# Splits before squares, a later memory norm, and alpha x written by ScalarE: three edits to a two-block transformer kernel

## The chip, the cores and the metric

The kernel runs on one core of a Trainium2 chip. TensorE (PE) multiplies matrices into eight PSUM banks, VectorE (DVE) and ScalarE (ACT) work elementwise, GpSimd (POOL) does next to nothing here, and SyncE (SP) issues nearly all DMAs. The metric is device time in microseconds (us) of one execution; lower is better.

## What is computed

Batch 1, 256 tokens, width 1024, all in float32. The first block is a chain of residual steps, the second a chain of post-norm steps. Cut from the reference:

```python
# first block
h = h + 0.5 * swiglu(rms_norm(h, g_ffn1), w_ffn1_gate, w_ffn1_up, w_ffn1_down)   # 1024 -> 2816 -> 1024
u = rms_norm(h, g_mix) @ w_in            # two kinds of attention over u, then @ w_out, added to h
h = h + 0.5 * swiglu(rms_norm(h, g_ffn2), ...)
h = h + sigmoid(rms_norm(h, g_ple_in) @ w_ple_gate + b) * rms_norm(p @ w_ple_proj, g_ple_out)
# second block, two layers l = 0, 1
mem_n = layer_norm(mem, mem_ln_g, mem_ln_b)
y = hybrid_ab_mixer(x, ...) if l == 0 else multiscale_pool_mixer(x, ...)
x = layer_norm(ALPHA * x + y, ln_mix_g[l], ln_mix_b[l])
y = memory_cross_attention(x, mem_n, w_q, w_k, w_v, w_o)
x = layer_norm(ALPHA * x + y, ln_xa_g[l], ln_xa_b[l])
y = (silu(x @ w_gate) * (x @ w_up)) @ w_down
x = layer_norm(ALPHA * x + y, ln_ffn_g[l], ln_ffn_b[l])
```

## The kernel before

**The weight stream.** All weights are cut into blocks of 128 x 1024 numbers (512 KB), numbered in the order in which PE uses them. SP loads block b into one of four raw buffers (`w_raw`) as soon as the low part of block b - 4 is made. ACT copies it, rounded, to `w_hi` (`part_hi`, L529), DVE subtracts to get `w_lo` (`part_lo`, L1046), and PE multiplies three times per tile, hi x hi, hi x lo and lo x hi (`three`, L1852 to L1854). A block of a feed-forward is 12 matmuls of 512 columns. The ring of `w_hi` and `w_lo` also has four places, so ACT may split block b + 4 when PE is done with block b: `behind(b)` is that step on ACT and on DVE. The activations are split in the same way (`x_hi` and `x_lo`, `h_hi` and `h_lo`).

**What sets the order.** Each engine's program is written out by hand, in the order in which it runs; semaphores join them. An engine never takes a later instruction first.

**A feed-forward** (`token_ffn(f, b0)`, f = 0 to 3) goes over the 2816 hidden columns in six steps n. Step 0 runs blocks G0 (gate, four blocks) and U0 (up, four). Each later step n runs G(n) with `turn_h(n-1)` in its middle (the hidden part turned from tokens to features), the four down blocks D(n-1), and U(n). Gate products stand in banks 0 and 1, up products and turned parts in 2 and 3, the sum of the down products in 4 to 7. ACT does the sigmoid (`sig`), DVE the two products (`gated`, `hidden`).

**The start.** PE multiplies ones to pass the time (22 matmuls, L2251), turns x (L1972), and begins G0. ACT does: split of weight block 0, half 0 of `x_hi` (L554, with waits for DVE's `x_lo`, L1068), squares of half 0 (L561), split of block 1, half 1 of `x_hi`, squares of half 1, splits of blocks 2 and 3. DVE follows with `w_lo` and `x_lo`, and makes the token rms (`token_rstd`, L1125 on), for which it needs all squares, between `w_lo` of block 2 and of block 3.

**The memory norm** lies inside the first feed-forward. `mem_tok` is loaded from ACT's DMA queue at the end of the start. DVE's `memory_stats` (L1168 to L1178) stands right behind `gated(0)`, ACT's `memory_norm` (L576) in U0, PE's `turn_memory` (L2003, 16 transposes into banks 4 to 7) behind `turn_h(0)`, ACT's `memory_gain` (L582) behind it; PE waits for the gain before the first down blocks. The split of the result (`memory_hi`, `memory_lo`) and `rope_tables` stand in step 2.

**The last two feed-forwards** (f = 2, 3) take x from a layer norm. `ln_norm` leaves the normalised x, tokens on partitions, in `xs[:, :, 1, :]`; PE turns it (`ln_turn`, L1910, token half t = 0 then 1), ACT applies gain and bias (`ln_x`, L668). Of G0, the first two blocks are split ahead, and `token_turns` runs all of G0 for t = 0, then for t = 1, with `ln_turn(v, 1)` behind the third block of t = 0. ALPHA x enters the output sum on PE: `residual` (L1938) multiplies x by ALPHA times the identity, eight float32 matmuls a call, behind the down blocks of steps 1 and 2. `T_BANK` says which banks the turns use.

**The end.** After the last block PE turns t = 0 and t = 1 of the last norm; ACT applies gain and bias to feature chunks 0 to 3 of both halves, DVE (L1836) to 4 to 7, and SP stores the four quarters (L504).

## Time and profile before

| | us |
|---|---|
| median of 3 runs (1311.31 to 1312.6) | 1312.11 |
| the profiled execution, its device time | 1311.42 |
| its span, first to last instruction | 1309.6 |
| PE busy | 1283.6 |
| DVE busy | 855.8 |
| ACT busy | 654.8 |

The profiled execution's time is 1.8 us over its span, and 0.7 us under the median. The mean granted TensorE clock is 0.992 of full speed. In the views, L12 is line 12 of the kernel; a row of the timeline has its start, its length, the engine, the line, and in brackets the idle time before it with what ended it. xN at a row's end is a run of N like instructions told as one.

### The profile page before, as it was taken

To read this page: it belongs to the slowest core of one execution; us is meant where nothing else is said; L and a number is where in the kernel's file an instruction comes from. 1 tells how busy PE (TensorE), PEld (TensorE's weight loads), DVE (VectorE), ACT (ScalarE), POOL (GpSimd) and SP (SyncE) were. 2 spreads that over 40 slices of the span, in tenths; PEclk is the share of its full clock that TensorE was granted. 3 is DMA by queue.
4 is the path that set the end of the run, shared out by engine and by line. 5 is a ranking of instruction groups with operands and counts; after the bars stand their busy time and mean duration, and the time that the engine had idled before them with its cause. 6 is when DMAs were issued, how large, how long until landed. Compare 5 with 4: busy or idle time off the path is not lost.

```text
span 1309.6 us, 17902 instructions
## 1 busy us (share of the span) xinstructions
PE 1283.6 (98%) x7108; PEld 1113.8 (85%) x7108; DVE 855.8 (65%) x1435; ACT 654.8 (50%) x987; POOL 5.4 (0%) x7
## 2 busy tenths in 40 slices
PE   8999999999999999999999999999999999999997
PEld 7888888897788888899889897888888997888886
DVE  5665557878667565678988765654557665555555
ACT  5554446657474444453535645543445654634442
POOL 0000000000000000000000000000001000000000
PEclk9999999999999999999998999999999999999998
DMA  8555555552355555544424532655554442555551
GB/s 278 185 183 189 192 177 194 174 165 81 105 178 191 185 186 191 178 145 162 147 95 137 184 131 94 216 179 179 186 191 146 164 143 81 193 177 180 189 191 51
DMA packets 61570, 215.82 MB, mean 165 GB/s; under 512 B 6576, under 2 KB 9904, under 8 KB 61232
## 3 DMA queue, kind: packets, MB, share of 16 engines
q1 hardware_dynamic: 61056, 213.15, 49.2%
q10 hardware_dynamic: 432, 1.54, 0.4%
q8 instruction: 56, 0.92, 0.3%
q14 instruction: 26, 0.21, 0.1%
HBM read 213.62 MB, written 1.05 MB: 164 GB/s over the span
## 4 chain that ended last, share of the span: by engine, by line
PE 86%; DVE 10%; ACT 2%; DMA 1%; issue 1%; SPq 0%; DVEq 0%; ACTq 0%
PE bank L1852 25%; PE bank L1854 25%; PE bank L1853 25%; DVE arena L1669 3%; DVE w_lo L1046 2%; PE bank L2051 1%; PE bank L1938 1%; PE bank L1874 1%; PE bank L2189 1%; PE bank L2149 1%; DMA w_raw<-weights_d 1%; PE bank L2160 1%; ACT w_hi L529 1%; DVE tokst L1325 0%; PE bank L2181 0%
## 5 line engine op out<-in xcount | busy, mean ns | idle before, releaser
L1046 DVE TENSOR_TENSOR w_lo<-w_raw,w_hi 128x1024 fp32r<-128x1024 f32 x383 | 467.1, 1225 | 355.3 <-ACT w_hi L529 353.9
L529 ACT ACTIVATE w_hi<-w_raw 128x1024 fp32r<-128x1024 f32 x383 | 404.1, 1059 | 500.5 <-PE bank L1854 479.9
L1852 PE MATMUL bank<-w_hi,x_hi 128*128 128x512 f32 (+2 forms) x992 | 373.3, 376 | 7.2 <-DVE w_lo L1046 6.5
L1854 PE MATMUL bank<-w_hi,x_lo 128*128 128x512 f32 (+2 forms) x992 | 367.8, 371 | 0.0
L1853 PE MATMUL bank<-w_lo,x_hi 128*128 128x512 f32 (+2 forms) x992 | 367.7, 371 | 0.0
L1852 PEld LDWEIGHTS bank<-w_hi,x_hi 128*128 128x128 f32 x992 | 187.6, 189 | 40.6 <-DVE w_lo L1046 7.6
L1854 PEld LDWEIGHTS bank<-w_hi,x_lo 128*128 128x128 f32 x992 | 187.6, 189 | 31.6
L1853 PEld LDWEIGHTS bank<-w_lo,x_hi 128*128 128x128 f32 x992 | 187.8, 189 | 30.4
L1852 PE MATMUL bank<-w_hi,h_hi 128*128 128x512 f32 (+1 forms) x364 | 142.3, 391 | 0.0
L1853 PE MATMUL bank<-w_lo,h_hi 128*128 128x512 f32 (+1 forms) x364 | 141.3, 388 | 0.0
L1854 PE MATMUL bank<-w_hi,h_lo 128*128 128x512 f32 (+1 forms) x364 | 141.3, 388 | 0.0
L1852 PEld LDWEIGHTS bank<-w_hi,h_hi 128*128 128x128 f32 x364 | 68.3, 188 | 14.7 <-DVE h_lo L1064 1.2
L1854 PEld LDWEIGHTS bank<-w_hi,h_lo 128*128 128x128 f32 x364 | 68.3, 188 | 14.0
L1853 PEld LDWEIGHTS bank<-w_lo,h_hi 128*128 128x128 f32 x364 | 68.4, 188 | 13.5
L1852 PE MATMUL bank<-x_hi,w_hi 128*128 128x256 f32 x256 | 74.3, 290 | 2.3 <-DVE arena L1698 0.9
L1853 PE MATMUL bank<-x_lo,w_hi 128*128 128x256 f32 x256 | 72.4, 283 | 0.0
L1854 PE MATMUL bank<-x_hi,w_lo 128*128 128x256 f32 x256 | 72.4, 283 | 0.0
L1852 PEld LDWEIGHTS bank<-x_hi,w_hi 128*128 128x128 f32 x256 | 49.0, 192 | 3.1 <-DVE arena L1698 1.1
L1669 DVE SCALAR_TENSOR_TENSOR arena<-arena,prm 128x256 f32<-128x256 f32 x120 | 50.0, 477 | 0.5
L1853 PEld LDWEIGHTS bank<-x_lo,w_hi 128*128 128x128 f32 x256 | 49.1, 192 | 0.2
L1854 PEld LDWEIGHTS bank<-x_hi,w_lo 128*128 128x128 f32 x256 | 49.1, 192 | 0.0
L1874 PE MATMUL bank<-xs,w_raw 128*128 128x256 f32 x192 | 43.0, 381 | 0.2 <-DVE xs L1633 0.2
(311 smaller groups left out, 1461.1 us busy)
## 6 DMA issues: line engine op xcount, KB each, us to landing
w_raw<-weights_d SPq DMA_DIRECT2D x395, 512.0 KB, 3.3
arena<-weights_d SPq DMA_DIRECT2D x4, 512.0 KB, 6.1
arena<-late_d SPq DMA_DIRECT2D x1, 1056.0 KB, 5.8
xs<-x_d SPq DMA_DIRECT2D x2, 512.0 KB, 6.1
kv_mem<-mem_d ACTq DMA_DIRECT2D x1, 1024.0 KB, 7.5
out_d<-xs SPq DMA_DIRECT2D x4, 256.0 KB, 2.8
cst<-cst_d SPq DMA_DIRECT2D x1, 671.0 KB, 10.4
arena<-pT_d ACTq DMA_DIRECT2D x1, 256.0 KB, 2.6
```

Source lines behind the costliest of these rows:

```text
L529: nc.scalar.activation(w_hi[:, slot(b), :], w_raw[:, b % RAW, :], ACT.Copy).then_inc(hi_ready, 1)
L1046: nc.vector.tensor_tensor(w_lo[:, slot(b), :], w_raw[:, b % RAW, :], w_hi[:, slot(b), :].bitcast(F32), ALU.subtract).then_inc(lo_ready, 1)
L1669: ins = nc.vector.scalar_tensor_tensor(conv[:, c, :], src, w, conv[:, c, :], ALU.mult, ALU.add)
L1852: nc.tensor.matmul(out, wh, xh, start=start, stop=False, skip_group_check=True)
L1853: nc.tensor.matmul(out, wh, xl, start=False, stop=False, skip_group_check=True)
L1854: return nc.tensor.matmul(out, wl, xh, start=False, stop=stop, skip_group_check=True)
L1874: ins = nc.tensor.matmul(out, w_raw[:, b % RAW, k * P:(k + 1) * P], x[:, k, 0, :], start=k == 0, stop=k == TILES - 1)
L1938: nc.tensor.matmul(PB[banks[t]][:, c % 4 * P:c % 4 * P + P], xs[:, c, 0, t * P:(t + 1) * P], res_i, start=False, stop=False, skip_group_ch ...
L2051: ins = nc.tensor.transpose(PB[2 + k][:, at:at + P], hf[:, t, (2 * k + j) * P:(2 * k + j + 1) * P], ident)
L2149: ins = nc.tensor.matmul(half(n % 2, t), xq[:, 2 * h + k, t * P:(t + 1) * P], k_mem[l][:, 2 * h + k, :], start=k == 0, stop=k == 1)
L2160: ins = nc.tensor.transpose(PB[2 + n % 2][:, k * S + t * P:k * S + (t + 1) * P], e_buf(n)[:, 0, t, k * P:(k + 1) * P], ident)
L2189: ins = nc.tensor.matmul(o[:, c * S:(c + 1) * S], v_mem[l][:, k, at:at + P], pt_buf(n)[:, k, :], start=k == 0, stop=k == 1)
```

## The change

1. **The start.** ACT splits weight blocks 1, 2 and 3 and all of `x_hi` first, then makes all four squares. DVE makes `w_lo` of block 3 before `token_rstd(0)`.
2. **Loads.** `mem_tok` is now loaded by SP, ahead of block 8, and `cst` ahead of block 12 (it was issued behind the first four blocks).
3. **The memory norm.** `memory_stats` moves behind the second block of D(0), `memory_norm` behind the second block of U(1). `turn_memory` comes in two halves of eight transposes, into banks 2 and 3, in the middle of D(1) and of D(2), with a wait for `f_hl`; ACT's gain comes in two halves behind it, and PE waits for each half before U(2) and U(3). `rope_tables` moves to step 3, the split of the result to step 4.
4. **ALPHA x of the last two feed-forwards.** PE's `residual` is gone there. DVE makes x in token form from the normalised x: four products with rows of the gain and four sums with rows of the bias (`residual_rows`), before `gated(0)`. ACT writes ALPHA times the four parts into banks 4 to 7 (`residual_in`), behind `sig(0)` and before the split of G1's first block; the first down blocks wait for it and add to it. The rows (1 MB for each layer) are loaded by SP ahead of G1's first block. The turns of t = 1 of the norms ahead (v = 6, 9) use banks 2 and 3 instead of 4 and 5, so PE waits there until ACT has read t = 0.
5. **The end.** ACT applies gain and bias to all eight chunks of t = 0 before its part of norm t = 1, then to chunks 0 to 3 of t = 1; DVE does only chunks 4 to 7 of t = 1.
6. In `weighted`, a start flag is set once for both halves of a bank.

```diff
-        T_BANK = {5: (0, 2, 4, 5), 6: ((2, 3), (4, 5)), 7: (0, 1, 4, 5), 8: (4, 5, 0, 1), 9: ((2, 3), (4, 5)),
+        T_BANK = {5: (0, 2, 4, 5), 6: ((2, 3), (2, 3)), 7: (0, 1, 4, 5), 8: (4, 5, 0, 1), 9: ((2, 3), (2, 3)),
...
-            sp.dma_start(cst[:], cst_d).then_inc(cst_in, 16)
             for b in range(RAW, NB):
+                if b == 2 * RAW:
+                    sp.dma_start(mem_tok, mem_d).then_inc(mem_in, 16)
+                if b == 3 * RAW:
+                    sp.dma_start(cst[:], cst_d).then_inc(cst_in, 16)
...
+                if b in (FIRST["ffn3"] + 6, FIRST["ffn4"] + 6):
+                    l = 0 if b < FIRST["ffn4"] else 1
+                    sp.wait_ge(t_ps, NH + XA_HEADS * (l + 1))
+                    sp.dma_start(ln_rows, row_d[l]).then_inc(row_in, 16)
...
+            def residual_in(f):
+
+                for h in range(2):
+                    for t in range(2):
+                        act.wait_ge(xt_ready, XT[f + 2] + 2 * h + t + 1)
+                        nc.scalar.activation(quarters(PB[Y_BANK[V_OUT[f]][2 * h + t]][:, :]), x_part(h, t, 1), ACT.Copy, scale=ALPHA
+                                             ).then_inc(y_set, 1)
...
                 sig(0)
+                if f >= 2:
+                    residual_in(f)
...
                 for i in range(AHEAD if f >= 2 else 0, 4):
                     behind(b0 + ffn_place("G", 0, i))
+                if f >= 2:
+                    residual_rows(f)
                 gated(0)
-                if f == 0:
-                    memory_stats()
...
+            def residual_rows(f):
+
+                dve.wait_ge(row_in, 16 * (f - 1))
+                dve.wait_ge(xt_ps, 16 + 4 * LN[V_IN[f]] + 4)
+                parts = [(x_part(h, t, 1), [quarters(ln_rows[:, k, h * HALF:(h + 1) * HALF]) for k in range(2)])
+                         for h in range(2) for t in range(2)]
+                for x, (g, _) in parts:
+                    mark(nc.vector.tensor_tensor(x, x, g, ALU.mult))
+                settle()
+                for x, (_, b) in parts:
+                    nc.vector.tensor_tensor(x, x, b, ALU.add).then_inc(xt_ready, 1)
...
+                if t and v != 10:
+                    pe.wait_ge(xn_ready, XN[v] + DC)
...
+                        if f >= 2 and n == 0 and jp == 0:
+                            pe.wait_ge(y_set, 4 * (f - 2) + 2 * h + 2)
...
                     for i in range(4):
-                        if f == 0 and n == 1 and i < 2:
-                            pe.wait_ge(mem_g, 4 * i + 4)
+                        if f == 0 and n in (2, 3) and i == 2:
+                            turn_memory(n - 2)
                         down(b1 + ffn_place("D", n - 1, i), n - 1, i // 2, i % 2)
-                    if f >= 2 and n < 3:
-                        residual(Y_BANK[V_OUT[f]][2 * n - 2:2 * n], n - 1)
                     up(n)
```

**On ACT at the start** (x_hi and w_hi are the rounded parts, the rows that read xs into xs are the squares). Before:

```order
L529 ACTIVATE w_hi<-w_raw 128x1024
L554 ACTIVATE x_hi<-bank,prm 128x256 x4
L561 ACTIVATE xs,tokst<-xs 128x4x128 x2
L529 ACTIVATE w_hi<-w_raw 128x1024
L554 ACTIVATE x_hi<-bank,prm 128x256 x4
L561 ACTIVATE xs,tokst<-xs 128x4x128 x2
L529 ACTIVATE w_hi<-w_raw 128x1024 x2
```

and after:

```order
L538 ACTIVATE w_hi<-w_raw 128x1024
L563 ACTIVATE x_hi<-bank,prm 128x256 x4
L538 ACTIVATE w_hi<-w_raw 128x1024
L563 ACTIVATE x_hi<-bank,prm 128x256 x4
L538 ACTIVATE w_hi<-w_raw 128x1024 x2
L570 ACTIVATE xs,tokst<-xs 128x4x128 x4
```

All four squares now stand behind the splits of blocks 1, 2 and 3.

**On DVE at G0 of the third feed-forward** (the last rows of the splits of x, the splits of U0's blocks, `gated(0)`, the splits of G1's first three, `hidden(0)`; the fourth feed-forward reads alike). Before:

```order
L1064 TENSOR_TENSOR x_lo<-xs,x_hi 128x2x128 x4
L1046 TENSOR_TENSOR w_lo<-w_raw,w_hi 128x1024 x3
L1225 TENSOR_TENSOR arena<-bank,arena 128x512 x2
L1046 TENSOR_TENSOR w_lo<-w_raw,w_hi 128x1024 x3
L1225 TENSOR_TENSOR arena<-bank,arena 128x512 x2
```

and after:

```order
L1082 TENSOR_TENSOR x_lo<-xs,x_hi 128x2x128 x4
L1064 TENSOR_TENSOR w_lo<-w_raw,w_hi 128x1024 x3
L1343 TENSOR_TENSOR xs<-xs,arena 128x4x128 x4
L1346 TENSOR_TENSOR xs<-xs,arena 128x4x128 x4
L1243 TENSOR_TENSOR arena<-bank,arena 128x512 x2
L1064 TENSOR_TENSOR w_lo<-w_raw,w_hi 128x1024 x3
L1243 TENSOR_TENSOR arena<-bank,arena 128x512 x2
```

Eight instructions stand before `gated(0)` and the splits of G1.

**On ACT at the end** (the norm's parts read bank and tokst, gain and bias read bank and prm). Before:

```order
L609 ACTIVATE h_hi<-bank 128x512
L529 ACTIVATE w_hi<-w_raw 128x1024
L660 ACTIVATE xs<-bank,tokst 128x4x128 x2
L668 ACTIVATE xs<-bank,prm 128x128 x8
L165 UNCONDITIONAL_BRANCH
```

and after:

```order
L626 ACTIVATE h_hi<-bank 128x512
L538 ACTIVATE w_hi<-w_raw 128x1024
L679 ACTIVATE xs<-bank,tokst 128x4x128
L687 ACTIVATE xs<-bank,prm 128x128 x8
L679 ACTIVATE xs<-bank,tokst 128x4x128
L687 ACTIVATE xs<-bank,prm 128x128 x4
L165 UNCONDITIONAL_BRANCH
```

The eight chunks of t = 0 now stand between the two parts of the norm, and four rows are new on ACT (DVE has four fewer).

## Rows read from the trace of the kernel before

**Rows 1.** From the page: busy time, share and instructions of PE, PEld, DVE, ACT

```profile
PE 1283.6 (98%) x7108; PEld 1113.8 (85%) x7108; DVE 855.8 (65%) x1435; ACT 654.8 (50%) x987; POOL 5.4 (0%) x7
```

**Rows 2.** Timeline of PE, start to 39 us: four rows with idle time before them

```profile
15.15 0.50 PE L1852 MATMUL bank<-w_hi,x_hi 128*128 128x512 f32 x1 [1.31 <-DVE w_lo L1046]
...
19.93 0.50 PE L1852 MATMUL bank<-w_hi,x_hi 128*128 128x512 f32 x1 [1.77 <-DVE w_lo L1046]
23.64 0.50 PE L1852 MATMUL bank<-w_hi,x_hi 128*128 128x512 f32 x1 [0.65 <-DVE w_lo L1046]
38.41 0.47 PE L1852 MATMUL bank<-w_hi,x_hi 128*128 128x512 f32 x1 [0.87 <-DVE w_lo L1046]
```

**Rows 3.** Timeline of ACT and DVE, 11 to 41 us

```profile
11.56 0.62 ACT L561 ACTIVATE xs<-xs 128x512 f32<-128x512 f32 x1
12.79 1.05 ACT L529 ACTIVATE w_hi<-w_raw 128x1024 fp32r<-128x1024 f32 x1
13.87 1.23 DVE L1046 TENSOR_TENSOR w_lo<-w_raw,w_hi 128x1024 fp32r<-128x1024 f32 x1 [1.68 <-ACT w_hi L529]
17.58 3.89 ACT L529 ACTIVATE w_hi<-w_raw 128x1024 fp32r<-128x1024 f32 x4
19.80 0.15 DVE L1125 TENSOR_TENSOR tokst<-tokst 128x2 f32<-128x2 f32 x1
22.36 1.23 DVE L1046 TENSOR_TENSOR w_lo<-w_raw,w_hi 128x1024 fp32r<-128x1024 f32 x1
24.30 3.49 DVE L1046 TENSOR_TENSOR w_lo<-w_raw,w_hi 128x1024 fp32r<-128x1024 f32 x3
31.56 2.46 DVE L1168 BATCH_NORM_STATS2 tokst<-kv_mem 128x6 f32<-128x512 f32 x4
37.05 3.49 DVE L1046 TENSOR_TENSOR w_lo<-w_raw,w_hi 128x1024 fp32r<-128x1024 f32 x3
```

**Rows 4.** Timeline of PE around one `residual` of the third feed-forward

```profile
855.22 1.95 PE L1938 MATMUL bank<-res_i,xs 128*128 128x128 f32 x16
856.92 0.48 PE L1852 MATMUL bank<-w_hi,x_hi 128*128 128x512 f32 x1
```

**Rows 5.** Timeline of DVE and PE at U0 and G1 of the third feed-forward

```profile
821.67 2.59 DVE L1046 TENSOR_TENSOR w_lo<-w_raw,w_hi 128x1024 fp32r<-128x1024 f32 x2 [0.45 <-ACT w_hi L529]
821.67 0.39 PE L1852 MATMUL bank<-w_hi,x_hi 128*128 128x512 f32 x1
826.38 1.23 DVE L1046 TENSOR_TENSOR w_lo<-w_raw,w_hi 128x1024 fp32r<-128x1024 f32 x1
832.55 0.39 PE L1852 MATMUL bank<-w_hi,x_hi 128*128 128x512 f32 x1
```

**Rows 6.** Timeline, first feed-forward: four DVE, four ACT instructions of 512 elements, all in SBUF

```profile
82.96 2.49 DVE L1064 TENSOR_TENSOR m_lo<-kv_mem,m_hi 128x512 fp32r<-128x512 f32 x4
...
81.45 2.19 ACT L589 ACTIVATE m_hi<-kv_mem 128x512 fp32r<-128x512 f32 x4
```

**Rows 7.** DMA issues by line: KB each, median us from issue to landing

```profile
arena<-late_d SPq DMA_DIRECT2D x1, 1056.0 KB, 5.8
```

**Rows 8.** Timeline, third feed-forward: ACT's last of t = 0, and PE's turn of t = 1

```profile
811.02 0.79 ACT L668 ACTIVATE xs<-bank,prm 128x128 f32<-128x128 f32 x2
813.67 1.04 PE L1910 MATMUL bank<-ident,xs 128*128 128x128 f32 x8
```

**Rows 9.** The end: timeline of ACT, PE, DVE; landing of the stores; a stretch of 1 us

```profile
1302.62 2.90 ACT L668 ACTIVATE xs<-bank,prm 128x128 f32<-128x128 f32 x8
1302.77 1.92 PE L1910 MATMUL bank<-ident,xs 128*128 128x128 f32 x8 [2.98 <-ACT xs L660]
...
1304.73 1.36 DVE L1836 TENSOR_SCALAR xs<-bank,prm 128x128 f32<-128x128 f32 x4 [0.83 <-PE bank L1910]
...
DMA to landing us min/median/max: 2.4/2.8/3.1
...
1306.00:1307.00 1.00, 0.00 (x0) 0.00 (x0) 0.09 (x1) 0.00 (x0) 0.00 (x0) 0.50 0.99 286
```

The columns of the last row are: stretch, us, busy us of PE, PEld, DVE, ACT and POOL, granted clock, DMA share, GB/s.

More of the change, by code:

```diff
@@ L577, in memory_norm, with memory_gain @@
                                              bias=ln_m[:, t:t + 1]).then_inc(mem_xn, 1)
-            def memory_gain():
-                for c in range(DC):
+            def memory_gain(h):
+                for c in range(4 * h, 4 * h + 4):
                     act.wait_ge(mem_t, c // 2 + 1)
-                    nc.scalar.activation(mem_f[:, c, :], half(4 + c // 2, c), ACT.Identity, scale=col("mem_g", c),
+                    nc.scalar.activation(mem_f[:, c, :], half(2 + c // 2 % 2, c), ACT.Identity, scale=col("mem_g", c),
                                          bias=col("mem_b", c)).then_inc(mem_g, 1)
@@ L1019, in _ @@
             token_ffn(3, FFN4)
+            ln_x(10, 0, 0, DC)
             ln_norm(10, 1)
-            for t in range(2):
-                ln_x(10, t, 0, 4)
+            ln_x(10, 1, 0, 4)
         @block.vector
@@ L1266, in token_ffn @@
                     hidden_lo(n - 1)
-                    if f == 0 and n == 2:
+                    if f == 0 and n == 3:
+                        rope_tables()
+                    if f == 0 and n == 4:
                         memory_lo()
-                        rope_tables()
                     if f == 1 and n == 1:
@@ L1278, in token_ffn @@
                         behind(b1 + ffn_place("D", n - 1, i))
+                        if f == 0 and n == 1 and i == 1:
+                            memory_stats()
                         if f == 1:
@@ L2041, in up @@
                         pe.wait_ge(f_hl, FFN_LO_ALL * f + 2 * n)
+                    if f == 0 and n in (2, 3):
+                        pe.wait_ge(mem_g, 4 * (n - 1))
                     for i in range(DC * FFN_W[n] // BLK):
@@ L2087, in token_ffn @@
                     turn_h(n - 1)
-                    if f == 0 and n == 1:
-                        turn_memory()
                     gate(n, 2)
@@ L2189, in weighted @@
                             ins = nc.tensor.matmul(o[:, c * S:(c + 1) * S], v_mem[l][:, k, at:at + P], pt_buf(n)[:, k, :],
-                                                   start=k == 0, stop=k == 1)
+                                                   start=c == 0 and k == 0, stop=k == 1, skip_group_check=True)
                 ins.then_inc(o_ps, 1)
@@ L2700 @@
               "prm": small_parameters(x), "ident": np.eye(P, dtype=np.float32), "cst": constants(),
-              "late": np.concatenate([pool_bands(), np.broadcast_to(x["pool_scale_2"].reshape(1, D), (P, D))], 1), "weights": np.ascontiguousarray(weight_stream(x))}
+              "late": np.concatenate([pool_bands(), np.broadcast_to(x["pool_scale_2"].reshape(1, D), (P, D))], 1),
+              "ln_rows": np.stack([np.broadcast_to(np.stack([x[f"ln_xa_{k}_2"][l] for k in "gb"]), (P, 2, D)) for l in range(2)]), "weights": np.ascontiguousarray(weight_stream(x))}
     nc = bacc.Bacc("TRN2", target_bir_lowering=False, num_devices=1)
```

52 lines of the change are left out of this document (26 added, 26 removed).

## The prediction

> **What bounds the kernel now.** I read the page's busy times first: PE is busy for 1283.6 of 1309.6 us, DVE for two thirds, ACT for half [rows 1]. So an edit gains only where it shortens PE's own work, one of PE's few waits, or the two ends of the program. PE's timeline comes next, for its idle time: four waits for DVE's `w_lo`, 4.6 us together, lie in the first 39 us [rows 2]. In the middle of a feed-forward PE needs 832.55 - 821.67 = 10.88 us for the four blocks of U0 [rows 5], so 2.72 for a block, while DVE needs 1.23 and ACT 1.05 for its share of one [rows 3]. There each has some 1.5 us to spare per block.
>
> **The start.** Squares of one half cost ACT 1.23 us (11.56 to the split that follows at 12.79) [rows 3]. With them behind:
> - Block 1 is split from 11.56 instead of 12.79, DVE makes its `w_lo` from 12.64 (was 13.87) to 13.87, and PE, through with block 0 at 13.84, starts it at 13.9 instead of 15.15.
> - Block 2 is split two pairs of squares earlier, at 17.58 - 2.46 = 15.1. Its `w_lo` ends at 15.1 + 1.05 + 1.25 = 17.4 and PE starts it at 17.5, having waited 0.6 (it needs 3.0 us for a block here: 15.15 to 19.93, less the idle 1.77 [rows 2]).
> - Block 3 is split from 16.1, its `w_lo` is there at 18.6, and PE starts it at 20.5, when it is through with block 2. That was 23.64.
> - Block 4 is late next. The squares now run from 17.1 to 19.6. The rms behind them takes DVE 22.36 - 19.80 = 2.56 us, to 22.2; the small instructions up to the next split take 24.30 - 22.36 less 1.13, the pitch of a split, so 0.8. Its `w_lo` then runs from 23.0 to 24.25 [rows 3]. PE is free at 20.5 + 2.8 = 23.3 and waits 1.0. Before, it started this block at 26.4 (five blocks lie between 23.64 and 38.41 - 0.87, so 2.78 each). 2.1 us are gained here.
>
> The memory norm's move takes away the last wait of 0.87 before block 8 [rows 2], since `memory_stats` no longer stands ahead of its split: I expect that `w_lo` by 30.1, and PE asks for it at 24.3 + 4 x 2.78 = 35.4. The start of block 8 moves from 38.41 to 35.4: **3.0 us**. The loads that SP takes over are no bound here: `mem_tok` is issued at 18.6 behind weight block 7, and a load of 1056 KB landed in 5.8 us [rows 7]; blocks 6 and 7, issued at 17.4 and 18.6, are needed on PE only from 29.9 on.
>
> Further on the norm's pieces lie beside full PE work. The longest, DVE's `memory_stats` (31.56 to 37.05, 5.5 us [rows 3]), now stands behind a split while PE has about four blocks, 10.9 us, before it needs the next one; split, statistics and split take 1.1 + 1.2 + 5.5 + 1.2 = 9.0. Covered by 1.9; if that cover were gone, it would cost what is over. Two breaks of PE's stream for eight transposes in place of one for 16 cost 0.1. Nothing for the rest.
>
> **ALPHA x.** One `residual` costs PE 856.92 - 855.22 = 1.70 us, and the matmul behind it restarts 0.08 late (0.48 long [rows 4] instead of 0.39 [rows 5]): 1.78, four times: **7.1 us**, all on PE, which has no wait in these stretches.
>
> What comes in is beside PE, but on engines that PE follows. At the third feed-forward DVE is through with U0's last split at 821.67 + 2.59 = 824.26 [rows 5]. Four instructions of 512 elements in SBUF take 2.49 us together, 0.62 each [rows 6]; four products and four sums take 4.95, to 829.2. ACT must wait for each sum. Its last copy starts at 829.2; a write of 512 elements from ACT to PSUM is nowhere in this trace, so I bound it by the copy within SBUF, 0.6 [rows 6], and by no time at all, and take 0.6: 829.8. Only then does ACT split G1's first block (1.05), and DVE makes `w_lo` by 829.8 + 1.05 + 1.25 = 832.1. PE asks for it at 832.55 [rows 5]. So it fits by 0.4 us, where before it was 826.38 + 1.23, 4.9 us early. `gated(0)`, which with its wait fills at most 824.26 to 826.38 now, 2.1 us [rows 5], is done by 831.3 even so, before ACT's split of G1 is used. The next splits follow at 833.3 and 834.5 and are asked for at 835.3 and 838.0: the lag is worked off. I take **0** and keep 0 to 1.5 us for each of the two feed-forwards.
>
> A rule of the Trainium skill speaks against this. "VectorE: DVE Perf Modes", in the section on the TRN2 errata, gives (N + 151)/0.96 ns for a float32 tensor_tensor, 691 ns at 512; four times that is 2.76, and the four of [rows 6] took 2.49, because each starts before the one ahead of it has ended. If each of the eight took the page's time one after the other, they would take 5.5 us, and by it PE would wait 0.15 us in each feed-forward and the sum would be 0.3 us worse.
>
> The wait before the turn of t = 1 costs nothing: ACT ends t = 0 at 811.8, PE turns at 813.67 [rows 8]. Behind it on PE stands G0's last block, which needs x parts that come later anyway. The rows' load, 1 MB, is issued near 814 and lands near 820 by [rows 7]; DVE wants it at 824.2, and blocks queued behind it on SP are wanted later still.
>
> **The end.** PE's turn of t = 0 ends at 1302.77 - 2.98 = 1299.8. ACT, idle until the norm's second part (it ends where the eight of L668 begin, 1302.6), can take t = 0 from about 1299.3 on: eight chunks at 0.36 [rows 9] end at 1302.2. The norm's part on ACT starts 0.3 later, and so do PE's turn and DVE's last four chunks, which end at 1304.73 + 1.36 + 0.3 = 1306.4. A loss of 0.3. Against it stand the stores: now all four are issued within 2.4 us and the DMA engines are full at 286 GB/s [rows 9]; 1 MB at that rate is 3.7 us. Issue to landing is 2.4 us at best and 3.1 at worst; I take the worst for the last store now and the best after the change, when half the data has left before 1304. 0.3 lost, 0.6 to 0.7 gained: **0.3 us** gained, between 0.4 lost and 0.8 gained.
>
> **Sum.** 3.0 + 7.1 - 0.1 + 0.3 = 10.3, and the span becomes 1299.3, the profiled execution 1301.1 (1.8 over it). The median before is 0.7 above its profiled execution, so I forecast 1301.8 us for the median.
>
> **The rivals.**
> - *The start gives less.* DMA engines are near full in the first 15 us, and if blocks 6 and 7, with `mem_tok` behind them, land later than I think, or the rms chain stretches, PE waits again before block 8. For it: DVE's chain is the new bound with nothing to spare at block 4. Against: what is issued at 17.4 has 12 us. It would leave 1 of the 3.0 us: 1304.
> - *ACT and DVE at G1 are late.* The margin of 0.4 us comes out of seven steps in a row, each waiting for another engine. If each of DVE's eight takes a third longer than the rows' 0.62, by the way in which its operands lie, the chain is 1.6 us longer, and a slower last copy adds up to 0.4, and PE waits 1.2 to 1.6 us, twice: 1304 to 1305. Against: the sources are in SBUF, as in [rows 6].
> - *The first weights come earlier too*, with `cst` gone from behind them, and PE starts by up to 1.5 us sooner: 1300.3. Against: `cst` was issued last, behind what PE waits for.
> - *Slower.* DVE waits in order for the rows of gain and bias; behind it stand `gated(0)` and every split, so PE stands still soon after. The load reaches 10.3 us of loss in all, and so no gain, when PE waits 5.2 us in each feed-forward: the rows would have to land at 824.2 + 0.4 + 5.2 = 829.8, nearly 16 us after issue, where a load of the size took 5.8 [rows 7]. At 18 us after issue the kernel would take 1317.
> - *The change doesn't do what it says:* if PE's time for `residual` was cover for ACT or DVE, removing it uncovers them. In these steps both wait for PE by some 1.5 us per block, so I give it no more than half of the 7.1 us: 1305.
>
> **How the numbers follow.** Forecast 0.68, within 1300.0 to 1303.5 (the bounds of start, 2 to 3.6, and end). Start gives less 0.09, late at G1 0.12, earlier weights 0.05, slower 0.02, uncovered engines 0.04. A measurement of this kernel tells about 0.2%, 2.6 us, from no change. Range 1299.6 to 1305: it leaves out part of the earlier weights, the deep end of the stalls and the slower case. Faster by over 0.2% holds in all but the slower case and the worst sums of the others: 0.96; within 0.2% 0.02; slower 0.02.
>
> **What would show it.** Start: PE's row with a wait for `w_lo` near 24.3 with 1.0 us of idle, and none near 38; block 8 at 35.4. ALPHA x: no rows of the residual after the third feed-forward starts, no wait of PE at G1's first block, and the `w_lo` before it done less than 1 us ahead. End: PE's last turn 0.3 later after the last block than now, last store landing in 2.4 to 2.5 us. I am wrong if PE shows waits of more than 1 us at the two G1, or new ones in D(1) to U(3) of the first feed-forward.

## The result, and the profile after

The changed kernel took 1298.72 us in the median of four runs (1298.31 to 1301.42), the kernel before, beside it, 1311.71: a ratio of 0.9906 with an interval of 0.9891 to 0.9920. That is 13.0 us less, and 3.1 less than the 1301.8 that I forecast; it lies just below my range. All executions of the study together give less: 1310.5 in the median of 79 executions of before (1309.0 to 1312.7), and 1299.9 in that of 14 of after (1298.3 to 1301.4), 10.7 apart.

The profiled execution took 1301.42 us, with a span of 1299.6; I had written 1301.1 and 1299.3. From the page of after, beside [rows 1]:

```profile
PE 1273.5 (98%) x7044; PEld 1104.1 (85%) x7044; DVE 864.3 (67%) x1447; ACT 660.8 (51%) x999; POOL 5.7 (0%) x7
```

PE is busy for 10.1 us less, DVE and ACT for 8.5 and 6.0 more, and PE still bounds. The waits of PE's timeline in the first 280 us of after, where [rows 2] had four:

```profile
17.23 0.50 PE L1883 MATMUL bank<-w_hi,x_hi 128*128 128x512 f32 x1 [0.55 <-DVE w_lo L1064]
24.00 0.50 PE L1883 MATMUL bank<-w_hi,x_hi 128*128 128x512 f32 x1 [1.02 <-DVE w_lo L1064]
```

These are blocks 2 and 4, forecast at 17.5 with 0.6 and at 24.3 with 1.0, and the wait at 38.41 is gone: between the second of these and 293 us PE has no wait over 0.1 us. DVE, then ACT, then DVE and PE again at G1 of the third feed-forward in after, where [rows 5] had `w_lo` of G1 at 826.38:

```profile
818.80 2.59 DVE L1064 TENSOR_TENSOR w_lo<-w_raw,w_hi 128x1024 fp32r<-128x1024 f32 x2 [0.45 <-ACT w_hi L538]
821.30 2.49 DVE L1343 TENSOR_TENSOR xs<-xs,arena 128x512 f32<-128x512 f32 x4
823.83 2.50 DVE L1346 TENSOR_TENSOR xs<-xs,arena 128x512 f32<-128x512 f32 x4
826.25 1.28 DVE L1243 TENSOR_TENSOR arena<-bank,arena 128x512 f32<-128x512 f32 x2
827.98 3.50 DVE L1064 TENSOR_TENSOR w_lo<-w_raw,w_hi 128x1024 fp32r<-128x1024 f32 x3 [0.45 <-ACT w_hi L538]
```

```profile
824.56 2.41 ACT L605 ACTIVATE bank<-xs 128x512 f32<-128x512 f32 x4 [2.03 <-DVE xs L1346]
826.90 4.11 ACT L538 ACTIVATE w_hi<-w_raw 128x1024 fp32r<-128x1024 f32 x4
```

```profile
829.69 0.39 PE L1883 MATMUL bank<-w_hi,x_hi 128*128 128x512 f32 x1
```

`w_lo` of G1's first block is there at 827.98 + 1.23 = 829.2, and PE takes it at 829.69 with no idle time in brackets. I had forecast a fit by 0.4 us; it fits by 0.5. DVE's row at 821.30 has no idle time either: the rows of gain and bias had landed, after 5.6 us.

What I had no line for is in the mixer of the second block. PE's timeline in after:

```profile
699.70 0.55 PE L1883 MATMUL bank<-m_hi,w_hi 128*128 128x256 f32 x1 [3.40 <-DVE w_lo L1064]
```

This wait of 3.40 us is not in the first profile of before. The stretches of 4 us around it (columns: stretch, us, busy us of PE, PEld, DVE, ACT and POOL, granted clock, DMA share, GB/s), first in before, then in after:

```profile
688.00:692.00 4.00, 4.00 (x36) 4.00 (x35) 3.89 (x6) 1.99 (x4) 0.00 (x0) 0.93 0.00 0
692.00:696.00 4.00, 4.00 (x20) 4.00 (x21) 3.59 (x18) 0.05 (x1) 0.00 (x0) 0.50 0.82 256
696.00:700.00 4.00, 4.00 (x26) 4.00 (x25) 3.65 (x18) 1.59 (x5) 0.00 (x0) 0.66 0.02 6
```

```profile
692.00:696.00 4.00, 4.00 (x36) 4.00 (x36) 3.66 (x18) 2.49 (x6) 0.00 (x0) 1.00 0.14 54
696.00:700.00 4.00, 0.60 (x4) 0.44 (x3) 3.72 (x12) 2.00 (x3) 0.00 (x0) 0.93 0.00 0
700.00:704.00 4.00, 4.00 (x24) 4.00 (x24) 4.00 (x10) 1.53 (x4) 0.00 (x0) 0.64 0.66 230
```

DVE is busy nearly throughout in both. A stretch of a few us in which the granted clock is at its lower level of 0.50 (1.2 GHz instead of 2.4) is called a fall below. In before, the falls came ahead of DVE's `w_lo`, and PE was 1.0 us late for it (it began the block at 703.96, and 684.33 + 18.65 = 702.98 is when DVE would have let it, see below). In after it ran at 1.00, came early, waited, and had the low clock behind the wait instead.

Measured between like rows of the two first profiles, the 10.0 us of span come from here: 0.27 at ACT's first split (8.00 to 7.73, the landing of block 0), 3.2 in the rest of the start, 3.2 and 3.6 in the two feed-forwards, and 0.3 at the end; 0.6 were lost in the mixer.

### The profile page after: what moved, and what is told of

The parts are those of the page before. It is cut to its first block, busy times and chain, and to the rows that moved or that the text cites. A ratio compares the mean times of both kernels' runs of the same rounds, so it can differ in the third digit from the quotient of the medians.

```text
span 1299.6 us, 17803 instructions
## 1 busy us (share of the span) xinstructions
PE 1273.5 (98%) x7044; PEld 1104.1 (85%) x7044; DVE 864.3 (67%) x1447; ACT 660.8 (51%) x999; POOL 5.7 (0%) x7
## 4 chain that ended last, share of the span: by engine, by line
PE 85%; DVE 11%; ACT 2%; issue 1%; DMA 1%; SPq 0%; DVEq 0%; ACTq 0%
PE bank L1883 25%; PE bank L1885 25%; PE bank L1884 25%; DVE arena L1702 3%; DVE w_lo L1064 3%; PE bank L2087 1%; PE bank L1905 1%; PE bank L2223 1%; PE bank L2183 1%; PE bank L1971 1%; DMA w_raw<-weights_d 1%; ACT w_hi L538 1%; PE bank L2194 1%; PE bank L2215 0%; ACT xs L570 0%
```

## The experiments

The open question was where a gain beyond my sum of 10.3 us came from. My first theory was the clock in the mixer, the rival a term of the sum that is too small.

**The parts.** After unedited; before with ALPHA x alone; after without it; after with the old order of the start; after with the old memory norm. Of the edits, the core lines:

```diff
# alpha_only: before, with (the two methods are those of the change)
+                if f >= 2:
+                    residual_in(f)
...
+                if f >= 2:
+                    residual_rows(f)
...
-                    if f >= 2 and n < 3:
-                        residual(Y_BANK[V_OUT[f]][2 * n - 2:2 * n], n - 1)
# no_alpha: after, with these undone
# no_start: after, with
             x_hi_of(0, 0, 4)
+            act.wait_ge(x_in[0], 32)
+            x_square(0, 0)
             part_hi(1)
             x_hi_of(0, 4)
+            act.wait_ge(x_in[1], 16)
+            x_square(0, 1)
             part_hi(2)
             part_hi(3)
-            act.wait_ge(x_in[0], 32)
-            x_square(0, 0)
-            act.wait_ge(x_in[1], 16)
-            x_square(0, 1)
...
             part_lo(2)
+            token_rstd(0)
             part_lo(3)
-            token_rstd(0)
# no_memory: after, with
                 gated(0)
+                if f == 0:
+                    memory_stats()
...
-                        if f == 0 and n in (2, 3) and i == 2:
-                            turn_memory(n - 2)
```

In no_memory the loads of `mem_tok` and `cst` are also back where they were.

> The changed kernel, unedited, to see what another execution of it looks like. Its profiled execution had a span of 1299.6 us, other executions 1296.5 and 1297.3. Theory 1, the clock: in the mixer of the second block (640 to 705 us) the granted TensorE clock fell in that execution (0.61 to 0.96 in eight us, 0.64 in four more), and where it does not fall the kernel ends some 2 to 3 us sooner; a profiled execution of 1296.5 us shows a clock of 1.00 from 640 to 705, and nothing else differs. Theory 2, a term of the sum was too small: 2.5 to 3 us are gained in every execution somewhere else (start, ALPHA x or end), and the timelines of the two executions differ by one wait that has nothing to do with the clock.

> Only the part on ALPHA x of the last two feed-forwards; start, memory norm and end as before. The sum says 7.1 us less than before. Theory 1: the mixer lies where it lay before, so its clock behaves as before, and it is 7 us and no more. Theory 2: 9.5 to 10 us if this part is the one that was priced too low.

> The change without the part on ALPHA x: the order at the start, the memory norm and the end are as changed. The sum says 3.0 + 0.3 - 0.1, so 3.2 us less than before. Theory 1: the mixer lies 3.3 us earlier, just as in the changed kernel, so the clock can do the same to it: 5.5 to 6.3 us less in most executions. Theory 2, with the start priced too low: the same 6 us in all executions, and the gain is seen ahead of 600 us.

> The changed kernel with the old order at the start (squares between the splits, rms before the low part of block 3). The sum says that this order is worth 2.1 of the 3.0 us of the start and the move of the memory norm 0.9, so the time is 2.1 us over that of the changed kernel. Theory 1: the mixer then lies 1.2 us earlier than before instead of 3.3, and the clock may fall in other executions than with the changed kernel, so 2 to 5 us over. Theory 2: 2.1.

> After, but with the memory norm where it was: memory_stats behind gated(0), the norm in U0, all 16 turns in step 1, its load from ACT's queue and cst behind the first four blocks. My sum says 0.9 of the start's 3.0 us goes with it (the wait before block 8), less 0.1 for the second break of the stream: 1300.7 beside 1299.9 of after. Rival: cst out of the way of the first weights makes block 0 arrive 0.3 us earlier, and this goes too: 1301.0, with ACT's first split back at 8.0 us instead of 7.73.

| kernel | median, us (executions) | ratio to before, 95% | against the before beside it, us |
|---|---|---|---|
| after_again | 1299.87 (1299.51 to 1300.55) | 0.9916 (0.9903 to 0.9930) | -11.3 |
| alpha_only | 1303.45 (1302.21 to 1304.63) | 0.9943 (0.9931 to 0.9955) | -7.7 |
| no_alpha | 1307.50 (1305.08 to 1307.80) | 0.9971 (0.9959 to 0.9982) | -3.7 |
| no_start | 1301.95 (1301.24 to 1302.63) | 0.9932 (0.9919 to 0.9944) | -9.2 |
| no_memory | 1300.72 (1299.42 to 1302.47) | 0.9927 (0.9915 to 0.9939) | -10.1 |

The parts add up: 7.7 + 3.7 = 11.4 beside 11.3. With 3.7 for no_alpha, its theory 1 (5.5 to 6.3) is out. The old order of the start costs 2.1 us, as forecast. The old memory norm costs 0.8 to 1.2 in the medians, where my sum had 0.9 less 0.1; the executions of no_memory and after_again overlap, so this part is carried by the wait in its trace more than by its time. The rival that `cst` holds up the first weights falls: ACT's first split stood at 7.61 in no_memory, at 7.33 in no_start, and between 7.3 and 8.1 in all profiles, with either order of loads. What no_memory brings back, on PE:

```profile
36.50 0.47 PE L1880 MATMUL bank<-w_hi,x_hi 128*128 128x512 f32 x1 [1.08 <-DVE w_lo L1062]
```

The first theory had said that these traces would differ in the clock, and they do (below), yet no part shows a gain that it alone explains.

**The cover at G1.** Four more products on DVE in each `residual_rows`:

```diff
                 settle()
+                for k, (x, (g, b)) in enumerate([parts[0], parts[2], parts[1], parts[3]]):
+                    if k >= 2:
+                        dve.wait_ge(vec_chain, chain[0] - 1)
+                    mark(nc.vector.tensor_tensor(g, x, b, ALU.mult))
                 for x, (_, b) in parts:
```

> After, with four more products of 512 elements on DVE in each residual_rows, between the products and the sums; their results are used by nothing. By my chain the margin at G1's first block is 0.45 us (w_lo ends at 829.2, PE asks at 829.7 in the trace of after), and four at 0.62 add 2.5 us, so PE waits 2.0 us before G1 in each of the two feed-forwards: 4.1 us more than after, 1304.0. Rival (the cover is larger than the rows suggest, since w_lo of G1's first block is not what PE waits for last, or the stall is worked off): under 1 us, 1299.9 to 1300.9.

It took 1305.6 us (1304.75 to 1306.51), 5.7 over after_again, and PE's timeline has the two waits:

```profile
829.69 0.47 PE L1887 MATMUL bank<-w_hi,x_hi 128*128 128x512 f32 x1 [1.90 <-DVE w_lo L1064]
...
1128.78 0.47 PE L1887 MATMUL bank<-w_hi,x_hi 128*128 128x512 f32 x1 [1.90 <-DVE w_lo L1064]
```

2.5 us more on DVE made 1.90 of waiting, so the cover was 0.6; I had 0.4. The expected time was 1304.0, 1.6 less than it took. Behind the first of the two waits the granted clock fell, behind the second it stayed at 1.00:

```profile
828.00:832.00 4.00, 2.31 (x8) 1.92 (x9) 3.68 (x4) 3.13 (x4) 0.00 (x0) 0.86 0.34 119
832.00:836.00 4.00, 4.00 (x14) 3.11 (x14) 2.84 (x4) 1.06 (x1) 0.00 (x0) 0.71 0.91 308
```

From the turn of x to the pooling, the third feed-forward took 3.7 us longer than in w_lo_early (below), the fourth, to the last turn, 2.2. So a wait here costs its own length and some 0.3 us, and in one of these two cases 1.5 us of low clock on top: a price that my rivals "late at G1" and "slower" left out.

**Before, once more.** No edit.

> The kernel before, unedited, profiled once more. Theory 1 (the gain that my sum lacks is in what TensorE's clock does between 640 and 705 us, and that changes from one execution to the next): this profile shows another granted clock there than the first one (0.90 and 0.89 at 648 to 664 us, 0.63, 0.93, 0.50, 0.66 from 684 to 700), and where the fall at 648 to 664 is missing the span is about 1.5 us shorter, near 1308. Theory 2 (the clock belongs to the program's order): the same falls at the same places and a span of 1309.6 again. The median of more rounds should be 1311.1, 1 us below the one from which I counted.

Median 1310.36 (1309.00 to 1311.73, 11 executions), ratio 0.9997 (0.9989 to 1.0006), span 1308.0, so 1.6 us less than the first profile of the same program. The median is 0.7 under the 1311.1 that I expected. The fall near 654 was there again, so I was wrong about that place. Of the 1.6 us, 0.43 are the landing of block 0 (first split at 7.57), and 1.0 lie between the waits near 684 and the turn near 737 (684.33 to 737.39 is 53.1 us, here 683.82 to 735.89, 52.1), where one fall of the clock stood instead of two. PE's waits in before_again:

```profile
683.82 0.36 PE L1852 MATMUL bank<-m_hi,w_hi 128*128 128x256 f32 x1 [0.80 <-DVE w_lo L1046]
702.46 0.36 PE L1852 MATMUL bank<-m_hi,w_hi 128*128 128x256 f32 x1 [1.87 <-DVE w_lo L1046]
```

From the one wait to the other it is 18.64 us, and in after 699.70 - 681.04 = 18.66, with a low clock in between here and none in after: DVE sets this time, as long as PE's own work fits in.

**DVE's order in the mixer.** What follows the wait is one split that stands behind the whole norm of the convolution on DVE. It can stand ahead:

```diff
# DVE
                 mark(nc.vector.bn_aggr(ln_mv[t], ln_bn[t][:, 0:6]))
+            blk()
             settle()
...
                                     ).then_inc(conv_nd, 1)
-            blk()
             mem_blocks(2, 3)
# ACT
             mem_blocks(1, 3, 4)
+            mem_blocks(1, 4, 5)
             act.wait_ge(conv_stat, 1)
...
-            mem_blocks(1, 4, 5)
```

> After, and DVE splits the last of the four memory blocks of the mixer's stage right behind the two aggregates of the convolution's norm instead of behind the whole norm; ACT makes the split of the next block before it waits for that norm. Theory (DVE's chain of 688 to 703 us is what PE waits for there, 3.4 us near 699, and the low clock behind this wait costs 1.4 more): the wait of 3.4 us is gone or under 0.5, PE starts the output projection at about 702 instead of 704.2, when the first x_lo is there, and the kernel takes 2.0 to 2.5 us less than after: 1297.6. Rival (something behind this stage, the attention's softmax on DVE, sets the time anyway): within 0.5 us of after, 1299.9.

> The kernel w_lo_early beside after on one chip. In its profile the output projection of the mixer began at 702.37 instead of 704.19, and 1.5 us of low clock behind it took most of that back (residual at 706.78 instead of 707.01). Theory 1 (the low clock behind the remaining wait of 2.38 us comes in most executions, as it does behind after's wait of 3.40): 0.2 to 1.2 us less than after, which five rounds cannot tell from no change. Theory 2 (DVE's order alone sets the time): 1.8 to 2.3 us less, 1297.4.

> After, unedited, a third time. Theory (the stores of before are bound by their 1 MB at 286 GB/s, which hides a slow last turn; those of after begin when the last chunks are done, so that a turn at the low clock shows): if the last turn takes 1.1 us here, 5.8 us from its start to the end of the span, and the end is worth 0.75 us; if it takes 1.9, 6.25 and 0.3 us. Median 1299.5, as in the nine runs so far. Rival (the landing of the last store varies by itself): no relation between the two.

w_lo_early took 1298.36 us (1297.69 to 1299.97), ratio 0.9909 (0.9896 to 0.9923). On one chip with after, w_lo_early_again took 1298.44 (1297.98 to 1298.92), ratio 0.9910 (0.9896 to 0.9923), and after_third 1300.30 (1299.38 to 1301.12), ratio 0.9921 (0.9907 to 0.9934). The executions of these two do not overlap, and their medians are 1.9 us apart. Over all executions it is 1.5: 1298.4 in the median of the eight with the earlier split, 1299.9 in that of the 14 of after, of which the fastest took 1298.3. PE's timeline in w_lo_early and in w_lo_early_again:

```profile
698.89 1.09 PE L2537 MATMUL bank<-ident,xs 128*128 128x128 f32 x8 [0.17 <-ACT xs L985]
702.37 0.47 PE L1883 MATMUL bank<-w_hi,x_hi 128*128 128x512 f32 x1 [2.38 <-DVE x_lo L1082]
```

```profile
702.26 0.47 PE L1883 MATMUL bank<-w_hi,x_hi 128*128 128x512 f32 x1 [1.55 <-DVE x_lo L1082]
```

The wait of 3.40 is gone and the output projection starts at 702.3, where after_again started it at 704.19. Behind the 2.38 the clock fell (0.68 from 704 to 708) and took 1.5 us back; behind the 1.55 it did not, as a fall stood ahead of it, from 680 to 683.5.

How much of the 1.5 to 1.9 us is the order's own? The traces say 0.3 to 0.4, if executions with the clock alike are compared. From the wait near 681 to the next wait of 0.90 (on `x_lo`, near 739), w_lo_early_again needed 737.10 - 680.27 = 56.8 us, where kernels with the old order and a fall ahead need 57.2; w_lo_early needed 738.78 - 680.38 = 58.4, where those with the fall behind need 58.6 to 58.7 (table below). The rest of the difference between the two profiles of one chip is where the falls lay. Whether the earlier split makes the dear place of the fall rarer, two profiles can't tell: one of them had it.

**Work in PE's waits.** Matmuls that nothing reads, in the wait near 650 and in that near 699 (or 702). The two kernels named early have the order of w_lo_early and both fillings:

```diff
+                if n == 19:                      # *_fill650 and early_filled: 16, the others: 8
+                    for _ in range(16):
+                        nc.tensor.matmul(PB[1][:, 0:P], ones, ident, start=True, stop=True)
...
+            for i in range(28):                  # after_fill699: 28, after_fill_14: 14
+                nc.tensor.matmul(half(4, 0)[:, 0:P], ones, ident, start=True, stop=True)
             mem_blocks(1, 5, 6)
...
+            for _ in range(20):                  # early_filled: 20, early_fill_8_10: 10
+                nc.tensor.matmul(PB[2][:, 0:P], ones, ident, start=True, stop=True)
             token_out(5, AB_OUT, "ab_out", ...
```

> The kernel before, with 16 matmuls of 128 columns (ones times ones' like, into a free bank, read by nothing) in front of the last block of the input projection of the mixer, where PE waits 1.9 us for w_lo near 653. In both profiles of before the granted clock stood at 0.55 to 0.59 from 654 to 658 us, behind that wait; the same wait in four of the seven profiles of changed kernels had it too. Theory 1 (the idle time itself brings the low clock, and with it about 1.5 us, of which 0.8 is taken back from DVE's bound near 660): no wait over 0.4 us there, clock 1.00 from 648 to 664, the time 0.7 to 1.2 us less than before: 1310.0 beside 1310.9. Theory 2 (the low clock comes from something else at this place): the clock falls there in spite of the filling and the time is unchanged, or slower by the filling's overrun, 0.2.

> After, with the same 16 matmuls at the same place (near 650 here). Theory 1: the clock is 1.00 there in each execution; since only some executions of after showed the fall, it gains less than in before, 0.3 to 0.7 us: 1299.1 beside 1299.6. If before gains 0.5 more than after here, this is where my sum's missing gain was. Theory 2: no change in either.

> After, with 28 such matmuls (about 3.1 us) in front of the last memory block of the mixer, where PE waited 3.40 us for w_lo near 699 and ran the block behind it in 4.4 instead of 2.9 us at a granted clock of 0.61 to 0.64. Theory 1 (the idle time brings the low clock): the clock stays at 1.00 from 700 to 704, the first block of the output projection starts 1.4 us sooner (702.8 instead of 704.2), 1298.2. Theory 2 (the low clock comes anyway): still near 0.6 at 700 to 704, 1299.6.

> After with the earlier w_lo of the run w_lo_early, the 16 matmuls near 650, and 20 more in front of the output projection, where w_lo_early still waited 2.38 us for x_lo and then had a granted clock of 0.68 from 704 to 708. Theory 1: no low clock between 640 and 710, 1.4 us less than w_lo_early (1298.4) for the second filling and 0.3 to 0.5 for the first: 1296.6. Theory 2: as w_lo_early, 1298.4.

I had sized these wrongly, by counting a float32 matmul of 128 columns once where the trace has two rows for it: 28 of them took 6.4 us, 16 took 3.7, 20 took 4.6, and all overran their waits. before_fill650 took 1311.30 us, ratio 1.0007 (0.9998 to 1.0015); after_fill650 1299.82, 0.9920 (0.9907 to 0.9934); after_fill699 1301.66, 0.9936 (0.9922 to 0.9950); early_filled 1300.62, 0.9929 (0.9917 to 0.9942). In after_fill699 and early_filled no fall came from 640 to 710 at all. Hence the four in the right size:

> The kernel before, with 8 matmuls of ones (0.23 us each, 1.86 us together) in PE's wait of 1.89 us near 653. With 16 of them the clock stood at 1.00 from 640 to 668, where both profiles of before showed 0.55 to 0.59 from 654 to 658. Theory 1 (the low clock behind this wait is what before loses and after mostly not): no wait over 0.3 us near 653, clock 1.00 to 668, and 0.6 to 1.0 us less than before. Theory 2 (what follows is bound by DVE near 660 and 699 anyway, so that the clock here costs nothing in the end): within 0.4 us of before, with the waits near 660 and 702 longer by as much.

> After, with the same 8 matmuls in the wait near 650. Theory 1: 0.2 to 0.5 us less than after (a fall was in one of its two profiles). Theory 2: within 0.3 us of after.

> After, with 14 such matmuls (3.2 us) in the wait of 3.40 us near 699. With 28 they ran for 6.4 us, 2.9 longer than the wait, and the kernel's later events came only 1.5 us later, at a clock of 1.00. Theory 1 (the low clock behind this wait costs 1.4 us and is on the path): clock 1.00 at 700 to 704, no wait over 0.4 us, output projection at 702.8 instead of 704.2, time 1.2 to 1.5 us less than after: 1298.2. Theory 2 (DVE's x_lo or what is behind it takes the gain back): under 0.5 us less.

> After with the earlier w_lo, 8 matmuls in the wait near 650 and 10 (2.3 us) in the wait of 2.38 us before the output projection. Theory 1: no low clock from 640 to 710, about 1.4 us less than w_lo_early, which was 1.2 under after: 1297.0, 0.2% less than after. Theory 2: as w_lo_early, 1298.4.

| kernel | median, us | ratio to before, 95% |
|---|---|---|
| before_fill_8 | 1310.04 (1309.62 to 1311.40) | 0.9995 (0.9986 to 1.0003) |
| after_fill_8 | 1299.37 (1298.11 to 1299.82) | 0.9912 (0.9899 to 0.9926) |
| after_fill_14 | 1300.91 (1300.00 to 1304.60) | 0.9930 (0.9917 to 0.9942) |
| early_fill_8_10 | 1299.60 (1298.02 to 1300.22) | 0.9917 (0.9903 to 0.9930) |

None is a gain that stands clear of the spread: before_fill_8 is 0.6 us under its before, inside the interval, after_fill_8 equals after, and after_fill_14 is above it. Its trace does show 0.6 to 0.7 us, the low end of theory 1, for before_fill_8: from the first weight matmul to the wait near 683 it needed 683.50 - 10.75 = 672.75 us, the two profiles of before 673.4 and 673.5.

At the filled places themselves the clock stayed up; after_fill699, with no fall ahead, is the clean case. From 696 to 704 in after_fill_14, beside 0.93 and 0.64 in after:

```profile
696.00:698.00 2.00, 2.00 (x21) 2.00 (x20) 1.86 (x7) 1.04 (x2) 0.00 (x0) 1.00 0.00 0
698.00:700.00 2.00, 2.00 (x21) 2.00 (x20) 2.00 (x3) 0.96 (x2) 0.00 (x0) 1.00 0.11 27
700.00:702.00 2.00, 2.00 (x20) 2.00 (x18) 2.00 (x6) 1.54 (x4) 0.00 (x0) 1.00 0.86 272
702.00:704.00 2.00, 2.00 (x19) 2.00 (x18) 2.00 (x5) 0.78 (x1) 0.00 (x0) 1.00 0.65 225
```

But this execution doesn't show that the filling kept it up, since a fall had come ahead, from 686.5 to 690.5, as the rows below show. Behind it PE was late, and the wait left to fill was 1.9 us and not 3.4 (680.27 + 18.66 = 698.93 is when DVE let it, against 697.0 for the end of its own work). The 3.2 us of filling overran by 1.1: `w_lo` was there at 698.8, and PE took it at 700.01.

```profile
684.00:688.00 4.00, 4.00 (x33) 4.00 (x33) 3.89 (x6) 1.46 (x4) 0.00 (x0) 0.85 0.00 0
688.00:692.00 4.00, 4.00 (x27) 4.00 (x26) 3.59 (x18) 0.10 (x1) 0.00 (x0) 0.72 0.83 261
```

```profile
697.56 1.22 DVE L1064 TENSOR_TENSOR w_lo<-w_raw,w_hi 128x1024 fp32r<-128x1024 f32 x1
700.01 0.36 PE L1883 MATMUL bank<-m_hi,w_hi 128*128 128x256 f32 x1
```

So what a filling of the right size is worth where the wait is 3.40 us was not measured: 28 matmuls were too long, and 14 met a shorter wait in the profiled execution. early_fill_8_10 has no fall from 640 to 710 in its trace, and its median is still 1.2 us over the 1298.4 of w_lo_early, not the 1.4 under it that theory 1 wanted; the executions of the two overlap.

The low clock also came where no wait of PE stood within 5 us ahead of it, as here and in before_fill_8 (its waits here are at 663.29 and 683.50, 0.8 us each):

```profile
684.00:688.00 4.00, 4.00 (x37) 4.00 (x35) 3.75 (x10) 2.78 (x4) 0.00 (x0) 1.00 0.42 131
688.00:692.00 4.00, 4.00 (x30) 4.00 (x29) 3.93 (x7) 0.78 (x3) 0.00 (x0) 0.76 0.11 30
692.00:696.00 4.00, 4.00 (x29) 4.00 (x29) 3.59 (x20) 0.88 (x3) 0.00 (x0) 0.82 0.71 237
```

Over the 20 profiles the picture of this stage is this. The wait of 1.9 us near 650 stood unfilled in 14; in 6 of them the clock fell to between 0.50 and 0.73 for 3 to 4 us right behind it, in 8 it did not; in the 6 filled ones it never did. Near 699 the fall's place sets what the stage costs. In the 14 profiles with the old order and no filling here:

| low clock between 680 and 700 | profiles | PE's wait near 699 | from the wait near 681 to that near 739, us |
|---|---|---|---|
| one fall, 3.5 to 4 us | before_again, before_fill_8, no_alpha, after_fill_8, rows_plus4 | 1.8 to 1.9 | 57.2 to 57.3 |
| 7 to 7.5 us in one stretch | alpha_only, before_fill650 | none over 0.4 | 57.2 |
| 11 us in two stretches | before, no_memory, after_fill650 | none over 0.4 | 58.2 |
| none ahead, one fall behind the wait | after, after_again, after_third, no_start | 3.4 | 58.6 to 58.7 |

With none ahead, PE is early, waits 3.4 us for DVE, and then runs the block in 4.4 us instead of 2.9. With up to 7.5 us of low clock ahead, the lost time comes out of those 3.4 us and costs nothing; with 11 us of it, 1.0 us is over.

**The end**, read from all profiles. The time from PE's last turn to the end of the span was 6.81 us in before_again, with the turn itself in 1.09 us, and 6.83 in before, with the turn in 1.92 [rows 9]. In after it was 6.26 and in after_again 5.79:

```profile
1293.34 1.95 PE L1943 MATMUL bank<-ident,xs 128*128 128x128 f32 x8 [3.23 <-ACT xs L679]
```

```profile
1292.71 1.11 PE L1943 MATMUL bank<-ident,xs 128*128 128x128 f32 x8 [3.23 <-ACT xs L679]
```

Nothing has been changed between these two; the turn ran at 1.2 GHz in one and mostly at 2.4 in the other. Of the other kernels with the new end, the seven whose turn took 1.1 to 1.5 us needed 5.80 to 5.89, and those with 1.9 and more 6.26 to 6.30; after_third, with 1.78, needed 6.1, and after_fill650, with 1.68, 6.0. The five profiles with the old end needed 6.81 to 6.85, whether the turn took 1.09 us (before_again) or 1.92 to 1.97 (the other four). Why before does not feel it is in the stretches of before_again, and of after_again behind them:

```profile
1304.00:1305.00 1.00, 0.00 (x0) 0.00 (x0) 0.00 (x0) 0.00 (x0) 0.00 (x0) 0.50 1.01 291
1305.00:1306.00 1.00, 0.00 (x0) 0.00 (x0) 0.00 (x0) 0.00 (x0) 0.00 (x0) 0.50 1.01 289
1306.00:1307.00 1.00, 0.00 (x0) 0.00 (x0) 0.00 (x0) 0.00 (x0) 0.00 (x0) 0.50 1.03 288
```

```profile
1294.00:1295.00 1.00, 0.00 (x0) 0.00 (x0) 1.00 (x4) 0.91 (x3) 0.00 (x0) 0.50 0.00 0
1295.00:1296.00 1.00, 0.00 (x0) 0.00 (x0) 0.23 (x1) 0.00 (x0) 0.00 (x0) 0.50 0.13 38
1296.00:1297.00 1.00, 0.00 (x0) 0.00 (x0) 0.00 (x0) 0.00 (x0) 0.00 (x0) 0.50 1.00 286
```

Before, the stores of 1 MB fill the DMA engines without a gap, and the last chunks are done long before their turn on them. In after_again the engines stand nearly empty from 1294 to 1296 and wait for the chunks, so the turn's clock is on the path.

## Why the prediction came out as it did

- **The base failed.** "The median before is 0.7 above its profiled execution, so I forecast 1301.8 us for the median." That took 1312.1, the median of three executions, for the kernel's time. All 79 executions gave 1310.5. With the sum as it stands the forecast would have been 1310.5 - 10.3 = 1300.2. The miss of 3.1 us is made up so: 1.6 by the base, 0.4 by the sum, and 1.1 by the four executions of after, whose median, 1298.72, is that much under the median of all 14. The last part is luck, and so was the base: of medians of three drawn from the 79, 95% lie between 1309.5 and 1311.8. The medians of before beside the other kernels, each of 9 to 15 executions on one chip, were 1309.8 to 1311.2. The 13.0 us of the result are therefore more than the change is worth.
- **The range failed with it.** Its lower end, 1299.6, had room for an earlier first weight only. One program's executions spread over 3.7 us (before) and 3.1 (after); a median of three strays by 1.1 to 1.2 us, and the forecast had one in its base and one in what was measured, so some 1.5 us at either side were needed (an estimate). None of my cases held it.
- **The sum held**: 10.3, measured 10.7 in the medians and 10.0 in the two first profiles. Two things that it lacked offset each other in part: the mixer lost 0.6 to 1.4 us, and the end gave up to 0.5 more. That they did is luck. Its parts were right. *Start*: 3.0; measured 3.2 between the first profiles without the landing's 0.27, and 2.5 between before_again and after_again, where the wait at block 8 was 0.49 and not 0.87, and PE's first block began 0.26 later after the change though ACT's first split did not. The two waits that I named came where I put them. The second break for the memory turns, 0.1 in the sum, shows no cost. *ALPHA x*: 7.1; measured 3.6 for each feed-forward (DVE in alpha_only was 1.7 us ahead of before at 824, 5.3 at 950 and at 1123, 8.9 at 1248), so 7.2, and 7.7 in the medians. Each of the two G1 has no wait.
- **The end's term was mis-sized**, 0.3 instead of up to 0.8. I took "the worst for the last store now and the best after the change"; the turn in [rows 9] was one at 1.2 GHz, which before hides and after does not. With a turn of 1.1 us the end gives 6.83 - 5.8 = 1.0, less the 0.25 by which the turn starts later. The 0.3 came true in after itself, whose turn was slow.
- **The margin at G1** was the step that I doubted most, and it came out at 0.5 to 0.6 for 0.4. *Late at G1* did not happen, nor did *slower* or *the change doesn't do what it says*. The rule from the Trainium skill ("VectorE: DVE Perf Modes", TRN2 errata, (N + 151)/0.96 ns, 691 ns at 512) would have had PE wait 0.15 us if the eight ran one after the other. The trace agrees with the time of one, 0.69 us, but not with that use of it: the next starts 0.60 us after the one ahead, and eight took 2.49 and 2.50 us, so they overlap as those in [rows 6] do. ACT's copies into PSUM follow DVE's sums one by one, which sets the pace of the four in 2.41 us; the last was 0.60 long itself, the upper bound that I took, and the split behind it started 0.54 after the copy's start.
- **First weights earlier**: a landing between 7.3 and 8.1 in every kernel, which the change does not move. The profile of before had it late.
- **New waits.** I had said that I was wrong if waits appeared in D(1) to U(3) or at G1; none did. The new wait was 400 us behind the edited start, in the mixer, and it costs the 1.5 us of low clock behind it. The theory that this is where a gain beyond the sum came from is not borne out: the stage lost 0.6 us in after beside the first profile of before and 1.4 beside before_again, and filling the waits changed no median beyond its interval, with the reserve that the wait of 3.40 us never had a filling of its size.

What stays open: why the low clock comes ahead of DVE's bound in some executions and behind it in others. The program alone does not decide it. All four profiles of before (two of them with a filling) had it ahead, the three of after behind; but up to some 690 us five more profiles are of the same program as after, and of these rows_plus4, after_fill_14 and w_lo_early_again had a fall between 680 and 700, w_lo_early and after_fill699 none. That after's faster executions (spans of 1296.5) have it ahead is likely, since rows_plus4 needed 1.4 us less for the stage than after did; no profile of such an execution was taken.

## What to carry to other kernels

Read the base from as many executions as you will compare with: a sum of terms that is right within 0.4 us is worth little on a median that is 1.6 off, and the range has to hold that as well. When a term rests on one row at a pipeline's end, see at which clock PE ran there and who hides it now, since the edit may remove what hid it. And where an engine that is not the bound sets one stretch (DVE for 18.7 us here), look at it after every gain elsewhere: moving one split ahead of a norm gave 1.5 to 1.9 us in the medians, of which the traces show 0.3 to 0.4 to be the order's own. Compare two traces only where the clock fell at like places.

## What the runs showed of the hardware

- A wait of PE costs more than its length at times: 1.90 us of idle time were followed by 0.86 and 0.71 of clock and 1.5 us of loss at 829, and by nothing at 1129, in one execution.
- Low clock in front of another engine's bound is free up to the slack there: 3.5 to 7.5 us of it between 680 and 700 cost nothing (57.2 us for the stage in seven profiles), 11 us cost 1.0.
- A float32 matmul of 128 columns with both operands float32 took 0.23 us (28 in 6.42, in 56 rows), and eight transposes 1.09 us at 2.4 GHz (before_again) and 1.97 at 1.2 (no_alpha).
- A float32 `tensor_tensor` of 512 elements on DVE was 0.69 us long, and the next one started 0.60 us after it.
- Stores of 256 KB kept the DMA engines full at 286 to 291 GB/s, and landed 2.8 us after issue in the median then; after the change, with empty engines ahead of the last ones, it was 2.3.
